# Seventeen fillers ahead of the first transposes of a hybrid decoder layer, and one behind each half tile

## What is computed

```python
def decoder_layer(x, ...):
    mix, new_conv, new_ret = token_mixer(rmsnorm(x, norm_mix), ...)
    h = x + mix
    h = h + moe(rmsnorm(h, norm_ffn), w_router, b_router, w_up, b_up, w_down, b_down)
    return h, new_conv, new_ret

def token_mixer(xn, ...):
    proj = xn @ w_in                      # 1024 -> 7 x 512: xc gB gC q k v g
    ...                                   # short convolution, retention, gate
    y = jnp.concatenate([a_out, r_out], axis=-1) @ w_out
```

## Time and profile before

| | |
|---|---|
| median of 3 timed runs | 1089.9 us (1089.86 to 1089.92) |
| the profiled execution's own time | 1088.76 us |
| its span, first to last instruction | 1086.9 us |
| TensorE busy | 1064.6 us, 98% of the span |
| VectorE / ScalarE busy | 33% / 14% |
| read from HBM | 427 MB, 396 GB/s over the span |

### The profile page before, as it was taken

How to read it: one execution, slowest core, us unless ns; L and a number is a source line. 1 busy time by engine, 2 the same in 40 slices (tenths; PEclk the granted TensorE clock), 3 DMA queues, 4 the chain that set the end, 5 groups by cost and what they waited for, 6 DMA issues and landing times.

```text
span 1086.9 us, 13159 instructions
## 1 busy us (share of the span) xinstructions
PE 1064.6 (98%) x5670; PEld 446.8 (41%) x5671; DVE 358.8 (33%) x569; ACT 152.7 (14%) x302; POOL 12.1 (1%) x28
## 2 busy tenths in 40 slices
PE   8999999999999999999999999999999999999997
PEld 6888764333333333333333333333333333333332
DVE  3455534322222222222222222223332222232234
ACT  2121144111111101111111111011111101001113
POOL 1000000000000000000000000000000000000002
PEclk9999999999999999999999999999999999999999
DMA  9875939999999999999999999999999999999994
GB/s 296 306 273 198 404 147 364 417 428 429 429 434 429 429 432 431 430 432 430 428 436 430 426 433 432 427 436 429 425 441 426 426 439 425 425 429 425 428 415 158
DMA packets 42923, 431.47 MB, mean 397 GB/s; under 512 B 4680, under 2 KB 20076, under 8 KB 25328
## 3 DMA queue, kind: packets, MB, share of 16 engines
q1 hardware_dynamic: 42256, 430.41, 94.6%
q10 hardware_dynamic: 608, 0.20, 0.1%
HBM read 427.00 MB, written 3.48 MB: 396 GB/s over the span
## 4 chain that ended last, share of the span: by engine, by line
PE 80%; DMA 19%; issue 0%; DVE 0%; ACT 0%; POOLq 0%; DVEq 0%; ACTq 0%; POOL 0%
PE bank L996 34%; PE bank L1015 15%; DMA ring_all<-in_w_up 14%; PE bank L675 9%; PE bank L1060 5%; DMA ring_all<-in_w_down 4%; PE bank L970 3%; PE bank L1007 2%; PE bank L788 2%; PE bank L978 2%; PE bank L988 1%; PE bank L637 1%; PE bank L1053 1%; PE bank L1072 1%; PE bank L796 1%; PE bank L1098 1%
## 5 line engine op out<-in xcount | busy, mean ns | idle before, releaser
L996 PE MATMUL bank<-ring_all,work 128*64 128x512 f32 x2048 | 484.6, 600 | 7.5 <-DMA ring_all<-in_w_up 7.4
L996 PEld LDWEIGHTS bank<-ring_all,work 128*64 128x64 f32 x2048 | 134.7, 136 | 257.2 <-issue 247.6
L1015 PE MATMUL bank<-ring_all,work 128*64 128x512 f32 x992 | 225.3, 596 | 1.4 <-DMA ring_all<-in_w_down 1.4
L1811 DVE TENSOR_TENSOR h_tok<-h_tok,bank 128x1024 f32<-128x1024 f32 (+1 forms) x67 | 81.7, 1220 | 236.8 <-PE bank L1060 230.9
L1015 PEld LDWEIGHTS bank<-ring_all,work 128*64 128x64 f32 x992 | 68.5, 137 | 130.5 <-issue 129.6
L675 PE MATMUL bank<-work,ring_all 128*128 128x264 f32 x384 | 86.9, 386 | 0.2 <-issue 0.2
L1781 DVE TENSOR_TENSOR work<-bank,bias_up 128x1024 f32<-128x1024 f32 x32 | 39.1, 1223 | 125.5 <-PE bank L1007 125.5
L675 PEld LDWEIGHTS bank<-work,ring_all 128*128 128x128 f32 x384 | 72.5, 190 | 12.4 <-issue 0.2
L1060 PE MATMUL bank<-work 64*128 64x512 f32 (+1 forms) x268 | 75.1, 637 | 0.0
L1798 DVE TENSOR_TENSOR work<-work 128x512 f32<-128x512 f32 x32 | 22.2, 692 | 108.6 <-ACT work L1399 108.5
L1383 ACT ACTIVATE work<-bank 128x264 f32<-128x264 f32 x32 | 12.5, 391 | 316.1 <-PE bank L988 316.1
(11 more groups left out here) (230 smaller groups left out, 544.3 us busy)
## 6 DMA issues: line engine op xcount, KB each, us to landing
ring_all<-in_w_up SPq DMA_DIRECT2D x44, 4096.0 KB, 35.0
ring_all<-in_w_down SPq DMA_DIRECT2D x22, 4096.0 KB, 35.9
ring_all<-in_w_up SPq DMA_DIRECT2D x32, 2048.0 KB, 27.4
ring_all<-in_w_down SPq DMA_DIRECT2D x15, 2048.0 KB, 39.2
ring_all<-in_w_up SPq DMA_DIRECT2D x16, 1024.0 KB, 9.7
ring_all<-in_w_in SPq DMA_DIRECT2D x13, 1024.0 KB, 5.1
ring_all<-in_w_down SPq DMA_DIRECT2D x10, 1024.0 KB, 9.8
ring_all<-in_w_out SPq DMA_DIRECT2D x4, 1024.0 KB, 10.6
```

The lines of the kernel that those rows point to most:

```text
L996: mm = pe.matmul(bank[half * CAP:(half + 1) * CAP, up_bank(n) + b, :].rearrange("q (k p) -> q p k", k=KT), x, src[:, half * FF + b * 512:h ...
L1015: mm = pe.matmul(bank[half * CAP:(half + 1) * CAP, Y, :], av[:, 2 * i + k, :], src[:, k * D + half * 512:k * D + (half + 1) * 512], start= ...
L1811: tt(rows, rows, bank[0:m, b:b + 2, :], ALU.add).then_inc(comb_added, 1)
```

## The change

VectorE fills 128 x 256 bf16 values with ones, in a stretch of `h_tok` that is written later in the kernel. TensorE multiplies this tile with itself, 128 x 128 stationary by 128 x 256 moving, into a part of bank 1 that nothing reads before the projection overwrites it: seventeen times before it waits for its first inputs, once behind each four transposes of the two prompt tiles, and twice more behind the last. That is 23 matmuls in all. No result is used.

```diff
+            filled = h_tok[:, 2, 512:640].bitcast(BF16)
...
+            fill_ready = sem("fill_ready")
...
+                def keep_warm(count):
+                    for _ in range(count):
+                        pe.matmul(bank[:, 1, 0:2 * P], filled[:, 0:P], filled, start=True, stop=True)
+
+                pe.wait_ge(fill_ready, 1)
+                keep_warm(17)
                 pe.wait_ge(ident_in, 16)
                 pe.wait_ge(norm_in, 16)
                 turn(bank[:, 2, 0:8], rows[0:8, :], 8).then_inc(norm_turned, 1)
...
                         mm.then_inc(xt_psum1, 1)
+                        if c < 2:
+                            keep_warm(1)
+                keep_warm(2)
...
+                nc.vector.memset(filled, 1.0).then_inc(fill_ready, 1)
                 nc.vector.memset(small[:, 6:14], 0.0).then_inc(eps_ready, 1)
```

## The result

| | before | after |
|---|---|---|
| median of 17 runs each, in alternation | 1090.02 us (1088.65 to 1093.45) | 1092.48 us (1090.45 to 1093.63) |
| ratio | | 1.0017, 95% interval 1.0011 to 1.0024 |
| the profiled execution's own time | 1088.76 us | 1091.92 us |
| mean granted clock of TensorE over it | 0.998 | 0.996 |

The changed kernel is slower, by 0.17%. The medians differ by 2.46 us; the ratio is above 1 beyond its interval and lies at the 0.2% that the prediction called its bound for telling a change. The time is above the predicted range, which ended at 1091.0.

What follows compares the result with a forecast made beforehand. TensorE holds 80% of the span, but `project(1)` waits for slot 0's reload, so 2.1 us won earlier pass on nought: 1088.8 us profiled, timed runs 1.1 above, forecast 1089.9 us, range 1088.6 to 1091.0.

Steps and rivals of the forecast that it cites:

- seventeen fillers: Ahead of TensorE's first inputs: 17 x 0.22 = 3.7 us, from about 1.1 to 4.8 us.
- they delay the first inputs: At TensorE's first transposes: no delay, since the DMA wait up to 5.08 us covers the fillers.
- small transposes end: Behind `project(0)`: the small transposes end at about 24.3 us in place of 26.4.
- `project(0)` starts: At the projection's first chunk: start at about 8.65 us in place of 10.09, a gain of 1.44 us.
- SyncE issues the reload: In SyncE's queue: weight slot 0's reload stays at 18.96 us, since nothing ahead of it waits for TensorE.
- reload lands: Ahead of `project(1)`: weight slot 0's reload lands at 18.96 + 7.6 = 26.56 us.
- TensorE idle ahead of `project(1)`: Ahead of `project(1)`: 2.1 us of saved work become 2.3 us of idle, with no gain passed on.
- from 26.6 on: From `project(1)` onward: everything as before, loads paced by TensorE and TensorE without a gap.
- the next load crowds the reload: Rival, at slot 0's reload: SyncE's next load, issued 2.1 us sooner, shares the queue; up to +3.1 us, 1093.0; 4%.
- the clock falls in the new idle time: Rival, ahead of `project(1)`: 2.3 us without work returns the clock to 1.2 GHz; +3.1 us, 1093.0; 3%.
- two signs of being wrong: Slot 0's reload landing more than 0.5 us away from 26.6, or a second granted-clock fall before the end.
- TensorE was late in those of before: Rival, at `project(1)` in timed runs: a later clock rise made TensorE set the start; up to 1.1 us back, 1088.8; 10%.

Runs made afterwards that it cites:

- next load held: Changed kernel with a SyncE wait, so that the load of slot 1 is issued only when the reload of slot 0 is in; 1091.91 us, ratio 1.0017.
- idle alone: Kernel before with one added wait ahead of `project(1)`, for VectorE's conversion of the router's weight, and no fillers; 1094.27 us, ratio 1.0032.
- changed again: The changed kernel unaltered, run once more on the chip of the held-back load, against the kernel before; 1093.52 us, ratio 1.0031.

## Why the prediction was wrong

| step of the prediction | predicted | profile after |
|---|---|---|
| seventeen fillers | 1.1 to 4.8 us, 0.22 each | 1.16 to 4.97, 3.81 us |
| they delay the first inputs | no | no: 5.13 [5.26 before, rows 2] |
| small transposes end | 24.3 | 25.16 |
| `project(0)` starts | 8.65 | 9.34; 8.65 in the second profile of it |
| SyncE issues the reload | 18.96, unmoved | 19.05 |
| reload lands | 26.56 | 27.79 |
| TensorE idle ahead of `project(1)` | 2.3 us, free | 2.72 us, and the clock falls |
| from 26.6 on | as before | 1.22 us late, and 1.44 us slower |

**What was right.** The cost of the fillers, their cover, and above all the reading that the gain would end at the reload of slot 0: the earlier trace rows showed TensorE starting 0.07 us after the landing, and the gain of 1.3 us did turn into idle time there (3.5 us in the second profile, where `project(0)` started at the predicted 8.65). It came to less in the first profile because the clock rose at 6.9 us, behind the first tile (4 transposes in 1.12 us, then in 0.60).

**What failed first: "from 26.6 on everything is as before", with its ground that the landing depends on loads queued ahead.** It depends as well on what else uses the sixteen DMA engines until the last part is in. The prediction looked at the order of SyncE's queue and found nothing moved. It did not ask who else has a queue. The page's part on queues has a line for instruction fetches, and the first of TensorE's could have been found at 25.28 us in the trace before; that it follows the code, so that 46 instructions ahead bring it forward, was to be thought of there. The rival "the next load crowds the reload" (4%) had the right place and the wrong cause: the lag was there before that load was issued. The sentence of the Trainium skill that the prediction set against it ("DMA: Bandwidth & Descriptors", section "Queues, rings and completion order") is about one ring, and against that rival it held. The same section of the Trainium skill says that a DMA engine goes round between its rings, a whole packet at a time; a 16 KB packet of 1.07 us in one engine's way fits that, and fifteen parts of sixteen that are not late do, too. Which part rode on the engine of the fetch the trace does not tell.

**What failed second: the rival "the clock falls in the new idle time", given 3%.** It was priced by one row: at the end of the kernel 3.5 us without work passed before the fall, and 2.3 was less. One fall shows how long the clock held once, not how long it holds. In the runs it fell 1.5 us (next load held), 2.2 (changed), 2.35 (idle alone) and 3.5 us (changed again) after the last record. By their mean clock it fell in nine runs of nine of the idle kernel and in sixteen of seventeen of the changed one, so the chance should have been most of the whole. Its size, +3.1 us, was too large for this profile: the stretch at 1.2 GHz lasted 3.4 us and cost 1.44, half of it less the idle moment at its head. With the next load held it lasted 6.8 us, and the 128 records took 31.55 - 28.72 = 2.83 us more.

The prediction had named two signs of being wrong, a landing more than 0.5 us away from 26.6 and a second fall of the clock. Both are in the profile: 27.79, and the fall at 27.4.

**The timed runs.** Both kernels' medians lie above their profiled executions. The prediction asked whether TensorE was late in those of before, and set that aside at 10%. The profiles give it more weight than that: without leading fillers the clock rose at 11.3 to 14.6 us from one execution to the next (11.26, 11.36, 12.27, 13.56, 14.56, 14.58), and with the later rises `project(1)` starts at 28.0 to 28.5, behind the reload. Then a raised clock would have had something to give. The rise in the timed runs is not on record, so that this is why they take 1.1 us more is argued, not shown.

The sum can be read in another way from the profiled executions: the time less the start of `project(1)` is 1061.9 to 1063.6 us in the six profiles whose clock does not fall behind 15 us and that wait for no later chunk, and 1064.0 to 1064.5 in the three with one fall of 3.4 us at `project(1)`. So an execution of this kernel is set in the main, to within 1.7 us, by when `project(1)` starts and by what the clock does there; some 0.5 us of the 3.16 between the two first profiles come behind 650 us and were not followed up.

## What to carry to other kernels

Time won ahead of a wait for a transfer is idle time, and on TensorE idle time can cost more than itself: price the fall of the clock there as likely, and put work that nobody needs into that gap, not only ahead of it. Before adding instructions to an engine, find its instruction fetches in the DMA queues and see which load they will meet once they come sooner. The gain appears only when what bounds the end of the stretch moves too; here that took the reload ahead of the small loads together with a start that never lets the clock drop.

## What the runs showed of the hardware

- TensorE's code comes in 16 KB packets, the first of 1.07 to 1.42 us in the fourteen profiles, over one of the sixteen DMA engines that carry the loads. When one fell near or behind the issue of a load, one of its sixteen parts (two or three in two profiles) landed late in most cases, by 0.4 to 2.2 us. Parts were also late without a fetch, by about 1 us in one profile from 7 us on. By the records run until then the first fetch came after 150 to 197 in kernels without added waits, and after 170 and 174 with the added instructions counted.
- The granted clock fell 1.5, 2.2, 2.35 and 3.5 us after the last record in four profiles, all at the same place of the program. It also fell at 8.0 us with TensorE busy for 2.01 of 3.3 us, and at 166 to 168 us after 4.75 busy of 5 us. What decides the last one stayed open.
- The first rise came anywhere from 11.3 to 14.6 us in six profiles without fillers ahead of the transposes, and at 4.1 to 6.9 us behind seventeen fillers.
- Ninety-two satisfied waits on TensorE made 46 instructions of two waits each, one in 106 ns.
